# First keys without the padding waits, heads in two halves, and twelve low parts by an adding DMA: a two-block fp32 network on one core

## The chip, the core and the metric

The kernel runs on one core of a Trainium2 chip. Five engines run side by side: TensorE (PE, matrix products; PEld is its weight load), VectorE (DVE), ScalarE (ACT), GpSimd (POOL) and SyncE (SP, which here only issues DMAs). They share an on-chip memory, wait for each other on semaphores, and each works through its own queue in order. TensorE writes to PSUM, eight banks of 512 fp32 columns. The metric is the device time of one execution in microseconds.

## The reference

Two transformer-like blocks over 512 positions of width 1024 (plus 16 meta tokens in front), batch 1, all in fp32. The first block mixes by retention and by sixteen stick-breaking heads, the second by a short convolution and a 31-tap convolution; each is followed by a gated feed-forward part.

```python
def stick_breaking(q, k, v):              # 16 heads of 64
    ...
        z = jnp.einsum('bhtd,bhsd->bhts', q_blk, k_pre) * scale
        ...
        log_not = jnp.where(valid, jax.nn.log_sigmoid(-z), 0.0)
        after = lax.cumsum(log_not, axis=3, reverse=True) - log_not
        a = jnp.where(valid, jnp.exp(jax.nn.log_sigmoid(z) + after), 0.0)
        outs.append(jnp.einsum('bhts,bhse->bhte', a, v_pre))

def mixer(xn, w_in, conv_a_w, conv_b_w, conv_b_bias, ln_b_gain, ln_b_bias, w_out):
    h = jnp.einsum("btd,de->bte", xn, w_in)
    b_gate, c_gate, h_a, glu_val, glu_gate = jnp.split(...)
    y_a = b_gate * causal_depthwise_conv(c_gate * h_a, conv_a_w)      # 3 taps
    g = glu_val * jax.nn.sigmoid(glu_gate)
    z = causal_depthwise_conv(g, conv_b_w) + conv_b_bias              # 31 taps
    y_b = jax.nn.silu(layer_norm(z, ln_b_gain, ln_b_bias))
    return jnp.einsum("bte,ed->btd", jnp.concatenate([y_a, y_b], axis=-1), w_out)
```

## The kernel before

Every fp32 product is made of three: an operand x is held as a rounded high part and a low part (x minus the high part), and `mm3` multiplies high by high, high by low and low by high (L497 to L499). The weights come in 140 units of 1 MB (128 x 2048 fp32), in a ring of two: SP loads unit u into `w_raw[u % 2]`, ScalarE copies it to `w_hi` (`split_hi`, L907), VectorE subtracts to get `w_lo` (`split_lo`, L1354), and TensorE waits for `w_lo_ready`. `split_hi(at, j)` and `split_lo(at, j)` are called for the unit two further on than unit j of the stage, once TensorE has done with unit j. `plan()` fixes which unit belongs to which stage. The order of work on each engine is the order of the calls in its block; nothing reorders it.

The first keys. VectorE splits units 0 and 1 (`first_split`), then scales the input and makes its low part tile by tile (`norm_split`), while TensorE runs small filler products (`keep_warm`) and then the keys and queries of the first head pair (`key_strip`). When the last low part stands, GpSimd zeroes the unused halves of the padded keys (four memsets, L476) and four more tiles (L479), counted by `keys_padded`. VectorE waits for all eight before `key_lo` and `query_lo`; TensorE then makes the scores of head 0 (`scores`, `meta_scores`).

The heads. For each of 16 heads: `scores` on TensorE, a softplus on ScalarE and VectorE that ends in `sp_hi`, `sp_lo` (column half 1, 768 columns of key blocks 1 to 3, is made before half 0, 512 columns of block 0), `logs` on TensorE (L641, cumulative sums over both), exponentials and `a_hi` on ScalarE, `a_lo` on VectorE, and `outputs` on TensorE. Between them TensorE works on weight units; in quads 1 to 3 VectorE also adds output strips to `acc` (`add_up`, L1522).

The convolution stage. Units of conv_b (4), conv_a (6), w_out2_a (2) and w_out2_b (2) pass through the ring. ScalarE takes each strip out of PSUM and then calls `split_hi`. VectorE runs 124 steps of the long convolution (`taps(n)`, 31 for each of four tiles, L1360, the first two of a pair L1869), the short convolution, and ten `split_lo` in between at fixed places. After w_out2_a TensorE runs 45 filler products, sums z over the channels (`mean`, L887), VectorE centres z, ScalarE squares it, TensorE sums the squares (`var`, L891), and so on to `y2`, which w_out2_b needs.

## Time and profile before

| | us |
|---|---|
| median of 3 runs | 1925.59 (1923.89 to 1926.1) |
| the profiled execution, its own time | 1925.76 |
| its span in the profile | 1924.0 |
| TensorE busy | 1868.7 (97%) |
| VectorE busy | 1139.6 (59%) |
| ScalarE busy | 708.6 (37%) |
| weight loads, 1 MB each, issue to landing | 4.9 (median) |

The profile is one execution. A row of the timeline gives when a run of like instructions starts, how long it takes in all, the engine, the line, the tiles, and in brackets how long the engine stood still before it and what released it. Times of the profile are counted from the start of the span. What lies outside the span is 1.76 us.

### The profile page before, as it was taken

The numbers are of one execution on the slowest core, as the hardware profiler recorded it, in microseconds if no ns is written. First come the engines' busy times: TensorE is split into PE (matmuls) and PEld (weight loads), VectorE is DVE, ScalarE is ACT, GpSimd is POOL, SyncE is SP. The second block draws the span as 40 slices with busy tenths as digits, with TensorE's granted clock in tenths as the row PEclk, the third lists the DMA queues.
The fourth block names the chain that finished last, engine by engine and source line by source line (L and its number), as shares of the span: only waits on it lengthen the run. The fifth ranks groups of instructions, "written<-read, shape, count | busy, mean of one in ns | idle before, by whom it ended". The sixth has DMA issues, their size and how long they took to land.

```text
span 1924.0 us, 24895 instructions
## 1 busy us (share of the span) xinstructions
PE 1868.7 (97%) x9978; PEld 1601.9 (83%) x9978; DVE 1139.6 (59%) x1418; ACT 708.6 (37%) x841; POOL 21.9 (1%) x21
## 2 busy tenths in 40 slices
PE   7999999899999999999899999999999999999996
PEld 7898989789898888988788888887998688888885
DVE  5566665653645647356565454547699765554546
ACT  4666666533323332333342222224323542222222
POOL 1000000010000000000000000000000000000000
PEclk8999999999999999999999999999999999999998
DMA  4011111122222222112513222221121212232221
GB/s 178 23 66 45 66 44 44 44 99 99 66 88 76 87 81 82 67 66 72 194 44 110 87 98 98 90 107 66 67 88 66 110 35 97 90 106 87 98 99 44
DMA packets 23186, 157.45 MB, mean 82 GB/s; under 512 B 2512, under 2 KB 2768, under 8 KB 5072
## 3 DMA queue, kind: packets, MB, share of 16 engines
q1 hardware_dynamic: 23120, 156.51, 23.3%
q8 instruction: 49, 0.80, 0.2%
q14 instruction: 17, 0.14, 0.0%
HBM read 154.40 MB, written 2.10 MB: 81 GB/s over the span
## 4 chain that ended last, share of the span: by engine, by line
PE 85%; DVE 8%; ACT 3%; issue 2%; DMA 1%; POOL 0%; SPq 0%; DVEq 0%; ACTq 0%; POOLq 0%
PE psum L497 27%; PE psum L498 26%; PE psum L499 26%; PE psum L641 2%; DVE z L1360 2%; PE psum L598 1%; DMA w_raw<-in_units 1%; DVE normed L1360 1%; ACT w_hi L907 1%; DVE w_lo L1354 1%; DVE h L1387 1%; ACT std L907 0%; PE psum L662 0%; PE psum L559 0%; DVE normed L1404 0%
## 5 line engine op out<-in xcount | busy, mean ns | idle before, releaser
L497 PE MATMUL psum<-X_hi,w_hi 128*128 128x512 f32 (+1 forms) x1632 | 588.7, 361 | 3.8 <-DVE w_lo L1354 2.3
L498 PE MATMUL psum<-X_lo,w_hi 128*128 128x512 f32 (+1 forms) x1632 | 582.1, 357 | 0.0
L499 PE MATMUL psum<-X_hi,w_lo 128*128 128x512 f32 (+1 forms) x1632 | 582.1, 357 | 0.0
L1354 DVE TENSOR_TENSOR w_lo<-w_raw,w_hi 128x2048 fp32r<-128x2048 f32 x134 | 306.9, 2291 | 155.8 <-ACT w_hi L907 155.8
L907 ACT ACTIVATE w_hi<-w_raw 128x2048 fp32r<-128x2048 f32 x134 | 255.8, 1909 | 373.5 <-PE psum L499 366.0
L497 PEld LDWEIGHTS psum<-X_hi,w_hi 128*128 128x128 f32 x1632 | 307.0, 188 | 52.2 <-issue 4.8
L498 PEld LDWEIGHTS psum<-X_lo,w_hi 128*128 128x128 f32 x1632 | 307.5, 188 | 45.2 <-issue 2.4
L499 PEld LDWEIGHTS psum<-X_hi,w_lo 128*128 128x128 f32 x1632 | 307.1, 188 | 44.2
L1522 DVE TENSOR_TENSOR acc<-acc,psum 128x512 f32<-128x512 f32 x216 | 142.1, 685 | 61.3 <-PE psum L499 60.8
L497 PE MATMUL psum<-M_hi,w_hi 128*128 128x512 f32 x352 | 137.0, 389 | 0.0
L498 PE MATMUL psum<-M_lo,w_hi 128*128 128x512 f32 x352 | 137.0, 389 | 0.0
L499 PE MATMUL psum<-M_hi,w_lo 128*128 128x512 f32 x352 | 137.0, 389 | 0.0
L497 PE MATMUL psum<-w_hi,X_hi 128*128 128x256 f32 x384 | 108.9, 283 | 0.0
L498 PE MATMUL psum<-w_lo,X_hi 128*128 128x256 f32 x384 | 108.7, 283 | 0.0
L499 PE MATMUL psum<-w_hi,X_lo 128*128 128x256 f32 x384 | 108.7, 283 | 0.0
L1802 DVE TENSOR_TENSOR gate_in<-psum,std 128x512 f32<-128x512 f32 x44 | 30.2, 691 | 122.1 <-PE psum L499 109.0
L907 ACT ACTIVATE silu_a<-gate_in 128x512 f32<-128x512 f32 x44 | 27.6, 631 | 168.9 <-DVE gate_in L1802 168.9
L1360 DVE SCALAR_TENSOR_TENSOR z<-glu,vec,z 128x512 f32<-128x512 f32 x120 | 80.5, 750 | 0.0
L499 PEld LDWEIGHTS psum<-M_hi,w_lo 128*128 128x128 f32 x352 | 66.1, 188 | 13.7
L498 PEld LDWEIGHTS psum<-M_lo,w_hi 128*128 128x128 f32 x352 | 66.1, 188 | 13.7
L497 PEld LDWEIGHTS psum<-M_hi,w_hi 128*128 128x128 f32 x352 | 66.1, 188 | 13.7
L497 PEld LDWEIGHTS psum<-w_hi,X_hi 128*128 128x128 f32 x384 | 73.8, 192 | 1.0 <-issue 0.2
...
## 6 DMA issues: line engine op xcount, KB each, us to landing
w_raw<-in_units SPq DMA_DIRECT2D x140, 1024.0 KB, 4.9
...
h<-in_xfm SPq DMA_DIRECT2D x1, 2112.0 KB, 7.4
...
```

The costliest lines, as they stand in the source:

```text
L497: nc.tensor.matmul(dst, w2[0], x2[0], start=first, stop=False, skip_group_check=True)
L498: nc.tensor.matmul(dst, w2[0], x2[1], start=False, stop=False, skip_group_check=True)
L499: m = nc.tensor.matmul(dst, w2[1], x2[0], start=False, stop=last, skip_group_check=True)
L598: m = nc.tensor.matmul(psum[0:rows, at.bank(s) + 1, 0:256], XM[:, k, meta], y[:, k, :], start=k == 0 and y is w[0], stop=k == DT - 1 and y ...
L641: m = nc.tensor.matmul(psum[:, 4 + KEY_BANK[b], c0:c0 + KEY_LEN[b2]], cmat[:, C_TRI if b2 == b else C_ALL, :], x[:, KEY_OFF[b2]:KEY_OFF[b2 ...
L907: return nc.scalar.activation(out_, in_, f, **kw)
L1354: v.tensor_tensor(lo, w_raw[at.ring(j)][:, :], as_f32(hi), ALU.subtract).then_inc(w_lo_ready, 1)
L1360: return v.scalar_tensor_tensor(out=out_, in0=in0, scalar=scalar, in1=in1, op0=op0, op1=op1)
L1387: v.tensor_tensor(h[:, k, META:FULL], h[:, k, META:FULL], normed[:, k % 2, 0:SEQ], ALU.add)\
L1522: v.tensor_tensor(dst[:, m, :], dst[:, m, :], strip_view(at.bank(s + n), SEQ), ALU.add)\
L1802: v.tensor_tensor(gate_in[:, c, :], strip_view(at.bank(s + c), SEQ), std[:, 0:SEQ], ALU.mult)\
```

## The change

Three parts. (1) First keys: VectorE splits unit 1 after `norm_split` instead of before; `key_lo` and `query_lo` no longer wait for GpSimd; only the small copies of the meta keys (`meta_keys_of`), now behind `query_lo`, and the scores wait for the first four memsets, and TensorE waits for all eight before the first quad. (2) Heads: `logs` and `outputs` go through key blocks 1, 2, 3, 0; blocks 1 to 3 wait for `sp_lo1` (`a_lo1`) alone, block 0 for `sp_lo0` (`a_lo0`); the exponentials, `a_hi` and `a_lo` are made in the same two halves. (3) Convolution stage: the low parts of twelve units (the third unit of conv_b to the second of w_out2_b) are no longer made by VectorE. ScalarE writes minus the rounded weights into `w_lo`, and GpSimd issues a DMA that adds `w_raw` to it; TensorE and the load of the next unit in the slot wait for that DMA's landing. The taps are portioned anew, two of the four sums over z stand between the units of w_out2_a, and 45 filler products become 8 and 8. The same wait (`weights_ready`) also replaces `w_lo_ready` in `unit`, `key_strip` and the feed-forward part; a few lines that only rename steps, semaphores and arguments are left out here.

```diff
 START, N_UNITS, N_STRIPS = plan()
+ADDED = (START["conv_b"][0] + 2, START["w_out2_b"][0] + 2)
+N_ADDED = ADDED[1] - ADDED[0]
+def added(u):
+    return type(u) is int and ADDED[0] <= u < ADDED[1]
...
         return w_hi[ring][:, :], w_lo[ring][:, :]
+    def lo_added(u):
+        return w_lo_added[u % 2], 16 * ((u - ADDED[0]) // 2 + 1)
...
         constant(rot[:, :, :].rearrange("p a b -> p (a b)"), 0)
-        def load(u, slot):
+        def load(u, slot, less):
             sync.wait_ge(w_hi_ready, u - 1)
-            sync.wait_ge(w_lo_ready, u - 1)
+            if type(u) is int and added(u - 2):
+                sync.wait_ge(*lo_added(u - 2))
+            else:
+                sync.wait_ge(w_lo_ready, u - 1 - less)
...
         sync.dma_start(meta2_f[:, :, :].rearrange("p a b -> p (a b)"), meta2).then_inc(x_loaded, 16)
-        loads(START["ffn0"][0] - 2, N_UNITS)
+        loads(START["ffn0"][0] - 2, ADDED[0] + 2)
+        for u in range(ADDED[0] + 2, N_UNITS):
+            load(u, u % 2, N_ADDED)
...
         for n in range(2):
+            if n:
+                for u in range(*ADDED):
+                    pool.wait_ge(w_neg_ready, u - ADDED[0] + 1)
+                    pool.dma_start(as_f32(w_lo[u % 2][:, :]), w_raw[u % 2][:, :], accum_op=ALU.add)\
+                        .then_inc(w_lo_added[u % 2], 16)
...
                 m.then_inc(*sig)
+        def weights_ready(at, j):
+            u = at.unit(j)
+            if added(u):
+                pe.wait_ge(w_hi_ready, u + 1)
+                pe.wait_ge(*lo_added(u))
+            else:
+                pe.wait_ge(w_lo_ready, u + 1 - (N_ADDED if at.u0 >= ADDED[1] else 0))
...
         def value_strip(at, j, s, half, meta):
-            pe.wait_ge(w_lo_ready, at.unit(j) + 1)
+            weights_ready(at, j)
...
         def logs(g):
-            pe.wait_ge(hd_dve.sem, hd_dve.at("sp_lo0", g))
-            for b in range(BLOCKS):
+            for b in (1, 2, 3, 0):
+                pe.wait_ge(hd_dve.sem, hd_dve.at("sp_lo1" if b else "sp_lo0", g))
...
                                              start=False, stop=False, skip_group_check=True)
-            m.then_inc(*hd_pe.step("logs"))
+                if b in (3, 0):
+                    m.then_inc(*hd_pe.step("logs1" if b else "logs0"))
...
         def outputs(t, r, g, p):
-            pe.wait_ge(hd_dve.sem, hd_dve.at("a_lo", g))
+            pe.wait_ge(hd_dve.sem, hd_dve.at("a_lo1", g))
                 pe.wait_ge(y_out, p)
-            for b in range(BLOCKS):
+            for b in (1, 2, 3, 0):
+                if b == 0:
+                    pe.wait_ge(hd_dve.sem, hd_dve.at("a_lo0", g))
                     split(a_hi, a_lo, ALL, slice(KEY_OFF[b], KEY_OFF[b] + KEY_LEN[b])),
-                    r == 0 and b == 0, False)
+                    r == 0 and b == 1, False)
...
         pe.wait_ge(quad_ready, 4)
-        pe.wait_ge(keys_padded, 8)
+        pe.wait_ge(keys_padded, 4)
         meta_scores(0, 0)
+        pe.wait_ge(keys_padded, 8)
...
         at = Place("w_out2_a")
-        for j in range(2):
-            unit(at, j, 4 * j, "R", SEQ, y2, None, counted(y2_ready, 0) if j == 0 else None)
-        keep_warm(45)
-        for t in range(CT):
+        def mean_of(t):
                              skip_group_check=True).then_inc(*c_pe.step(f"mean{t}"))
+        for j in range(2):
+            unit(at, j, 4 * j, "R", SEQ, y2, None, counted(y2_ready, 0) if j == 0 else None)
+            if j == 0:
+                mean_of(0)
+                mean_of(1)
+        keep_warm(8)
+        mean_of(2)
+        mean_of(3)
+        keep_warm(8)
...
             act.wait_ge(w_loaded[at.ring(j)], 16 * (at.loads(j) + 1))
+            u = at.unit(j)
+            if type(u) is int and added(u + 2):
+                a(w_lo[at.ring(j)][:, :], w_raw[at.ring(j)][:, :], ACT.Copy, scale=-1.0).then_inc(w_neg_ready, 1)
...
             a(sp_all_hi[:, :], sp[:, 0:SEQ], ACT.Copy).then_inc(*hd_act.step("all_hi"))
-            act.wait_ge(hd_pe.sem, hd_pe.at("logs", g))
-            for n, (bank, off, w) in enumerate(PARTS):
-                a(a_f[:, off:off + w], psum[:, 4 + bank, 0:w], ACT.Exp).then_inc(*hd_act.step(f"a_part{n}"))
-            act.wait_ge(hd_act.sem, hd_act.at("a_part2", g))
-            a(a_hi[:, :], a_f[:, :], ACT.Copy).then_inc(*hd_act.step("a_hi"))
+            for half, cols, parts in ((1, H1, (1, 2)), (0, H0, (0,))):
+                act.wait_ge(hd_pe.sem, hd_pe.at(f"logs{half}", g))
+                for n in parts:
+                    bank, off, w = PARTS[n]
+                    a(a_f[:, off:off + w], psum[:, 4 + bank, 0:w], ACT.Exp).then_inc(*hd_act.step(f"a_part{n}"))
+                act.wait_ge(hd_act.sem, hd_act.at(f"a_part{parts[-1]}", g))
+                a(a_hi[:, cols], a_f[:, cols], ACT.Copy).then_inc(*hd_act.step(f"a_hi{half}"))
...
         query_hi(0, at, 1)
+        act.wait_ge(w_lo_ready, 2)
...
             split_lo(at, 1)
-        for u in range(2):
-            first_split(u)
+        first_split(0)
         norm_split(0, 0, FULL, "pre_mix")
+        first_split(1)
...
                 .then_inc(*hd_dve.step("all_lo"))
-            dve.wait_ge(hd_act.sem, hd_act.at("a_hi", g))
-            v.tensor_tensor(a_lo[:, :], a_f[:, :], as_f32(a_hi[:, :]), ALU.subtract)\
-                .then_inc(*hd_dve.step("a_lo"))
+            for half, cols in ((1, slice(SEQ, PACKED)), (0, slice(0, SEQ))):
+                dve.wait_ge(hd_act.sem, hd_act.at(f"a_hi{half}", g))
+                v.tensor_tensor(a_lo[:, cols], a_f[:, cols], as_f32(a_hi[:, cols]), ALU.subtract)\
+                    .then_inc(*hd_dve.step(f"a_lo{half}"))
...
             ins.then_inc(strip_free, 1)
-            if not (type(p) is int and p == 0):
-                dve.wait_ge(mk_pe.sem, mk_pe.at("m_scores", p - 1))
+            if type(p) is int and p == 0:
+                return
+            dve.wait_ge(mk_pe.sem, mk_pe.at("m_scores", p - 1))
+            meta_keys_of(t, at, s)
+        def meta_keys_of(t, at, s):
...
         dve.wait_ge(quad_ready, 4)
-        dve.wait_ge(keys_padded, 8)
         query_lo(0, at, 1, 0)
+        dve.wait_ge(keys_padded, 4)
+        meta_keys_of(0, at, 0)
...
                     .then_inc(y2_ready, 1)
-        b, ca = Place("conv_b"), Place("conv_a")
-        split_lo(b, 0)
-        split_lo(b, 1)
         dve.wait_ge(c_dve.sem, c_dve.at("glu1"))
-        taps(11)
-        split_lo(b, 2)
-        taps(13)
-        split_lo(b, 3)
+        taps(31)
         gated_linear(1)
-        taps(11)
-        split_lo(ca, 0)
-        taps(13)
-        split_lo(ca, 1)
+        taps(29)
         short_conv(0)
-        taps(5)
+        taps(2)
+        dve.wait_ge(c_dve.sem, c_dve.at("glu3"))
+        taps(6)
         y_a(0)
-        taps(3)
+        taps(2)
         y_a_lo(0)
-        split_lo(ca, 2)
-        taps(6)
-        dve.wait_ge(c_dve.sem, c_dve.at("glu3"))
-        split_lo(ca, 3)
-        taps(13)
-        split_lo(ca, 4)
+        taps(26)
         short_conv(1)
-        taps(4)
+        taps(8)
         y_a(1)
-        taps(1)
+        taps(2)
         y_a_lo(1)
-        split_lo(ca, 5)
             stt(z[:, t, :], psum[:, 4, :], -1.0 / WB, z[:, t, :], ALU.mult, ALU.add).then_inc(*c_dve.step(f"zc{t}"))
-        for j in range(2):
-            split_lo(Place("w_out2_a"), j)
```

VectorE at the first keys, before (`first_split(1)`, then `norm_split` to its last tile, then the first keys and queries):

```order
L1394 CAST w_hi<-w_raw 128x2048 [waits w_loaded1]
L1396 TENSOR_TENSOR w_lo<-w_raw,w_hi 128x2048 [waits w_hi_ready]
L1360 SCALAR_TENSOR_TENSOR normed<-h,vec,std 128x528 [waits x_in2,x_in3,x_in1,std_ready,x_in0,vec_in]
...
L1369 TENSOR_TENSOR X_lo<-normed,X_hi 128x528 [waits x_hi_ready] x2
L1481 TENSOR_TENSOR K_lo<-psum,K_hi 64x528 [waits keys_padded,qk_act,quad_ready,consts_in]
L1481 TENSOR_TENSOR K_lo<-psum,K_hi 64x528 [waits qk_act]
L1488 CAST KM_hi<-K_hi 128x64 [waits strip_free]
L1490 CAST KM_lo<-K_lo 128x64
L1360 SCALAR_TENSOR_TENSOR Q_lo<-psum,Q_hi 128x512 [waits qk_act]
```

and after:

```order
L1445 TENSOR_TENSOR w_lo<-w_raw,w_hi 128x2048 [waits w_hi_ready]
L1409 SCALAR_TENSOR_TENSOR normed<-h,vec,std 128x528 [waits x_in2,x_in3,x_in1,std_ready,x_in0,vec_in]
...
L1418 TENSOR_TENSOR X_lo<-normed,X_hi 128x528 [waits x_hi_ready] x2
L1443 CAST w_hi<-w_raw 128x2048 [waits w_loaded1]
L1445 TENSOR_TENSOR w_lo<-w_raw,w_hi 128x2048 [waits w_hi_ready]
L1531 TENSOR_TENSOR K_lo<-psum,K_hi 64x528 [waits qk_act,quad_ready,consts_in]
L1531 TENSOR_TENSOR K_lo<-psum,K_hi 64x528 [waits qk_act]
L1409 SCALAR_TENSOR_TENSOR Q_lo<-psum,Q_hi 128x512 [waits qk_act]
L1542 CAST KM_hi<-K_hi 128x64 [waits strip_free,keys_padded]
L1544 CAST KM_lo<-K_lo 128x64
```

The two instructions of `first_split(1)` moved from ahead of `norm_split` to behind it, the wait for `keys_padded` from the keys to the meta copies, and these behind the queries.

VectorE in the second half of the convolution stage, from the last tap group of the middle portion to the centring of z (`z<-psum`), before:

```order
L1360 SCALAR_TENSOR_TENSOR z<-glu,vec,z 128x512 [waits conv_step] x11
L1354 TENSOR_TENSOR w_lo<-w_raw,w_hi 128x2048 [waits w_hi_ready]
L1887 TENSOR_TENSOR u_in<-c_in,u_in 128x528 [waits strip_free]
...
L1360 SCALAR_TENSOR_TENSOR z<-glu,vec,z 128x512 [waits conv_step] x4
L1906 TENSOR_TENSOR c_in<-c_in,b_in 128x512 [waits c_dve,strip_free]
L1906 TENSOR_TENSOR c_in<-c_in,b_in 128x512 [waits c_dve]
L1360 SCALAR_TENSOR_TENSOR z<-glu,vec,z 128x512 [waits conv_step]
L1913 TENSOR_TENSOR y_lo<-c_in,y_hi 128x512 [waits c_act] x2
L1354 TENSOR_TENSOR w_lo<-w_raw,w_hi 128x2048 [waits w_hi_ready]
L1360 SCALAR_TENSOR_TENSOR z<-glu,vec,z 128x512 [waits conv_step] x44
L1360 SCALAR_TENSOR_TENSOR z<-psum,z 128x512 [waits c_pe]
```

and after:

```order
L1409 SCALAR_TENSOR_TENSOR z<-glu,vec,z 128x512 [waits conv_step] x26
L1942 TENSOR_TENSOR u_in<-c_in,u_in 128x528 [waits strip_free]
...
L1409 SCALAR_TENSOR_TENSOR z<-glu,vec,z 128x512 [waits conv_step] x8
L1961 TENSOR_TENSOR c_in<-c_in,b_in 128x512 [waits c_dve,strip_free]
L1961 TENSOR_TENSOR c_in<-c_in,b_in 128x512 [waits c_dve]
L1409 SCALAR_TENSOR_TENSOR z<-glu,vec,z 128x512 [waits conv_step] x2
L1968 TENSOR_TENSOR y_lo<-c_in,y_hi 128x512 [waits c_act] x2
L1409 SCALAR_TENSOR_TENSOR z<-glu,vec,z 128x512 [waits conv_step] x18
L1409 SCALAR_TENSOR_TENSOR z<-psum,z 128x512 [waits c_pe]
```

The low parts of the weights are gone from between the taps, and 18 taps stand where 44 stood.

TensorE from the end of a w_out2_a unit to w_out2_b (`psum<-z,ones` are the sums over z, `psum<-ones` the filler), before:

```order
L499 MATMUL psum<-y_hi,w_lo 128x512
L569 MATMUL psum<-ones 128x128 x45
L887 MATMUL psum<-z,ones 128x512 [waits conv_step] x4
L891 MATMUL psum<-sq,ones 128x512 [waits c_act] x4
L569 MATMUL psum<-ones 128x128 x30
L497 MATMUL psum<-y_hi,w_hi 128x512 [waits strip_free,y2_ready,w_lo_ready]
```

and after:

```order
L523 MATMUL psum<-y_hi,w_lo 128x512
L920 MATMUL psum<-z,ones 128x512 [waits conv_step] x2
L521 MATMUL psum<-y_hi,w_hi 128x512 [waits strip_free,w_lo_added0,w_hi_ready]
...
L523 MATMUL psum<-y_hi,w_lo 128x512
L601 MATMUL psum<-ones 128x128 x8
L920 MATMUL psum<-z,ones 128x512 [waits conv_step] x2
L601 MATMUL psum<-ones 128x128 x8
L934 MATMUL psum<-sq,ones 128x512 [waits c_act] x4
L601 MATMUL psum<-ones 128x128 x30
L521 MATMUL psum<-y_hi,w_hi 128x512 [waits strip_free,y2_ready,w_lo_added1,w_hi_ready]
```

Two sums moved ahead of the second unit; the waits for the weights now name the DMA's semaphore.

## Rows read from the trace of the kernel before

**Rows 1.** The page, part 1: busy us, share of span, instructions by engine.

```profile
PE 1868.7 (97%) x9978; PEld 1601.9 (83%) x9978; DVE 1139.6 (59%) x1418; ACT 708.6 (37%) x841; POOL 21.9 (1%) x21
```

**Rows 2.** Timeline, VectorE, first keys: start us, us, engine, line, op, [idle before].

```profile
19.12 1.44 DVE L1360 SCALAR_TENSOR_TENSOR normed<-h,vec,std 128x528 f32<-128x528 f32 x2
...
29.13 1.50 DVE L1369 TENSOR_TENSOR X_lo<-normed,X_hi 128x528 fp32r<-128x528 f32 x2
36.85 1.42 DVE L1481 TENSOR_TENSOR K_lo<-psum,K_hi 64x528 fp32r<-64x528 f32 x2 [6.22 <-POOL m_lo L479]
38.31 1.96 DVE L1488 CAST KM_hi<-K_hi 128x64 fp32r<-128x64 f32 x1
...
77.02 0.20 DVE L1488 CAST KM_hi<-K_hi 128x64 fp32r<-128x64 f32 x1
```

**Rows 3.** Timeline, ScalarE, GpSimd and TensorE, first keys.

```profile
16.19 0.65 ACT L907 ACTIVATE std<-std 128x528 f32<-128x528 f32 x1
...
33.66 0.60 ACT L907 ACTIVATE Q_hi<-psum 128x512 fp32r<-128x512 f32 x1
...
33.80 0.97 POOL L476 MEMSET K_lo<- 64x1056 f32 x1
...
15.25 5.52 PE L569 MATMUL psum<-ones 128*128 128x128 f32 x48
21.45 0.36 PE L497 MATMUL psum<-X_hi,w_hi 128*128 128x264 f32 x1 [0.67 <-DVE X_lo L1369]
...
41.18 0.77 PE L497 MATMUL psum<-Q_hi,K_hi 128*128 128x512 f32 x1 [8.12 <-DVE Q_lo L1360]
```

**Rows 4.** Windows: us, busy us PE PEld DVE ACT POOL, granted clock, DMA.

```profile
46.00:47.00 1.00, 1.00 (x5) 0.74 (x4) 0.00 (x0) 1.00 (x3) 0.00 (x0) 0.67 1.04 442
...
924.20:927.60 3.40, 1.11 (x5) 0.64 (x4) 2.77 (x2) 0.60 (x1) 0.00 (x0) 0.96 0.04 17
```

**Rows 5.** Waits of TensorE, whole span: us in total, times, longest.

```profile
PE psum L641 <- DVE sp_lo L1438: 4.2, 3, 1.4
```

**Rows 6.** Timeline, TensorE and VectorE, third head of quad 1.

```profile
177.91 0.50 PE L641 MATMUL psum<-sp_hi,cmat 128*128 128x512 f32 x1 [1.39 <-DVE sp_lo L1438]
187.34 0.44 PE L662 MATMUL psum<-sp_all_hi,cmat 128*64 128x512 f32 x1 [0.32 <-DVE sp_all_lo L1450]
...
183.79 0.69 DVE L1522 TENSOR_TENSOR acc<-acc,psum 128x512 f32<-128x512 f32 x1 [0.61 <-PE psum L499]
```

**Rows 7.** Timeline, VectorE and TensorE, convolution stage.

```profile
1384.23 2.29 DVE L1354 TENSOR_TENSOR w_lo<-w_raw,w_hi 128x2048 fp32r<-128x2048 f32 x1 [1.15 <-ACT w_hi L907]
...
1469.06 29.25 DVE L1360 SCALAR_TENSOR_TENSOR z<-glu,vec,z 128x512 f32<-128x512 f32 x44
...
1485.17 10.21 PE L569 MATMUL psum<-ones 128*128 128x128 f32 x90
1495.22 1.88 PE L887 MATMUL psum<-z,ones 128*128 128x512 f32 x4
```

**Rows 8.** Timeline, ScalarE, convolution stage.

```profile
1370.61 1.91 ACT L907 ACTIVATE w_hi<-w_raw 128x2048 fp32r<-128x2048 f32 x1
...
1381.78 0.61 ACT L907 ACTIVATE conv_sig<-psum 128x528 f32<-128x528 f32 x1 [5.00 <-PE psum L499]
...
1430.19 1.23 ACT L907 ACTIVATE y_hi<-c_in 128x512 fp32r<-128x512 f32 x2 [1.89 <-DVE c_in L1906]
...
1439.38 0.61 ACT L907 ACTIVATE c_in<-psum 128x528 f32<-128x528 f32 x1 [4.72 <-PE psum L499]
...
1487.78 1.28 ACT L963 ACT_TABLE_LOAD   x1
1500.44 1.23 ACT L907 ACTIVATE sq<-z 128x512 f32<-128x512 f32 x2 [11.38 <-DVE z L1360]
```

**Rows 9.** DMA issues of the program: count, KB each, median us to landing.

```profile
w_raw<-in_units SPq DMA_DIRECT2D x140, 1024.0 KB, 4.9
...
h<-in_xfm SPq DMA_DIRECT2D x1, 2112.0 KB, 7.4
```

22 lines of the change are left out of this document (12 added, 10 removed).

## The prediction, on record before the changed kernel was run

> **What bounds the kernel now.** I read the page first, then TensorE's waits, then the timelines around the three places that the diff touches. The page says who is the bound: TensorE is busy 97% of the span, VectorE 59%, ScalarE 37% [rows 1]. So work taken from VectorE is worth something only where TensorE stands still for VectorE, or runs filler in place of work. In the timelines the reader is to look at the brackets and at filler. Three such places are in reach. At the first keys TensorE stands still for 8.12 us until 41.18 [rows 3]. In the head pairs it waits three times for `sp_lo`, 4.2 us in all [rows 5]. After the convolution it finishes real work at 1485.2 and runs 10.2 us of filler, since VectorE's taps run on to 1498.3 [rows 7]; ScalarE waits 11.38 us for that, until 1500.44 [rows 8].
>
> **Part 1, the first keys.** `norm_split` begins at 19.12, behind `first_split(1)` [rows 2]. What it needs, std, is there at 16.19 + 0.65 = 16.84 [rows 3], so it moves up by about 2.2 us and its last low part ends at 28.4 instead of 30.6. TensorE's filler ends at 15.25 + 5.52 = 20.77 and the first key product waits 0.67 more for X_lo [rows 3]: from then on filler and not X_lo is late, so the key and query products end 0.65 earlier, at about 32.4. ScalarE's Q_hi, which ended at 34.26 [rows 3], ends at 33.6.
>
> The split of unit 1 now stands behind: its two instructions took 3.5 us (15.65 to 19.2, the gap in front of 19.12), so they run from 28.4 to 31.9 and end before the first K_hi is there (32.35). Then K_lo twice, 0.7 each, the second ending at 33.7, and Q_lo, 0.7, ends at 34.4. The four pads of the keys ended at 34.77 [rows 3]; GpSimd starts on the last X_lo, so 2.2 us earlier: 32.5, or 33.8 if its first memset waits for the 1.2 us copy of `first_split(1)`. Both lie before 34.4. The 6.22 us wait for GpSimd ahead of K_lo and the 1.96 us of the meta copy ahead of Q_lo [rows 2] are gone from the path. The scores start at about 34.5 instead of 41.18: 6.7 us.
>
> Then the clock. The trace shows half the full clock (1.2 instead of 2.4 GHz) while the scores run, until about 46.7: the second from 46 to 47 has a mean of 0.67 [rows 4]. From 41.18 to 46.7 are 5.5 us at half clock, 2.75 of them lost. TensorE had stood still for over 8 us. Now it stands still for 2.1 us only, and I take the clock as staying full: 2.3 us more (the same products end at 37.8 instead of 46.8). The counter-case is in the trace too: a stretch of 3.4 us with 1.11 us of work, before 927.6 [rows 4], was followed by half clock. Sum: 9.0 us with full clock, 6.5 to 7.3 if it falls. The load of unit 3 now waits for the later split of unit 1, until 31.9; with 4.9 us [rows 9] it lands at 37, long before ScalarE wants it (past 50). The wait for all eight memsets ends at about 36, behind it 37.8.
>
> The copies (CAST) and the memsets. KM_hi took 1.96 us beside GpSimd's memset of `acc`, and 0.20 at 77.02 without one [rows 2]: they hold each other up. The 1.2 us copy of unit 1 now meets the first pad; if it is the one that waits (0.97 us), Q_lo comes 0.7 later. That is in the range. The Trainium skill (SBUF — State Buffer, Who interferes with whom) says that the two engines share a port pair that one instruction holds for its whole length; the trace agrees.
>
> **Part 2, the heads.** A wait of 1.39 us [rows 6] ends when both halves of `sp_lo` stand. Half 0 takes 0.6 to 0.7 us of VectorE after half 1; `logs` on blocks 1 to 3 has 1.4 us of work before it wants half 0. So each wait shrinks by 0.7. The next wait of TensorE, 0.32 at 187.34, is on a chain of VectorE whose `acc` addition at 183.79 waited for TensorE itself [rows 6]; it moves along by 0.6. Three waits (quads 1 to 3), 0.6 each: 1.8 us. The additional instructions (one copy on ScalarE, one subtraction on VectorE per head) cost 0.1 us each, 16 times, and lie beside TensorE's weight units; no wait of TensorE over 0.2 us names `a_lo`. If they were on the path it would be a loss of 1.6, which the range holds.
>
> **Part 3, the convolution stage, if the DMAs are in time.** Ten splits of 2.29 us [rows 7] leave VectorE before the end of the taps, and so do seven short waits like the 1.15 ahead of one. Laid out again (taps 0.67 each, each block behind the strip that it waits for), the last tap ends at about 1478.5 instead of 1498.3. VectorE is then no longer late. What is late next: TensorE. It ends w_out2_a at 1485.2, plus two sums moved in between, 0.94 each [rows 7]: 1487.1. Then 8 fillers of 0.23, two sums, and z can be centred at 1490.9. But ScalarE is later still: its last strip moves by 1.9, and the negated copy adds 1.9 ahead of w_hi and the table load. That load ended at 1487.78 + 1.28 = 1489.06 [rows 8], and now ends at 1492.85. The squares started at 1500.44 and start at 1492.85: 7.6 us. From the squares on the chain is the same; the two splits that VectorE ran in it were hidden. The negated copy (1.9) in front of w_hi also delays one strip of w_out2_a by 0.2.
>
> **The adding DMA.** No row shows one. Its time T runs from the end of the negated copy to the release of TensorE. What T may be: ScalarE starts on a unit at 1370.61, TensorE has done with the next at 1381.7, just ahead of ScalarE's take at 1381.78 [rows 8]. 11.1 less 1.9 leaves 9.2 us. The tightest is the fifth unit of conv_a: ScalarE makes y_hi first, until 1431.4 (some 1 us earlier once VectorE is not behind), the copy ends at 1432.1, and TensorE wants the unit at 1439.3 [rows 8]: 7.2 us. One more has 8.4 us, the other six or seven about 9.2; the last two units have time to spare.
>
> Bounds of T: from below a plain load, 4.9 us [rows 9]. A 2112 KB load takes 7.4, so 2.3 of it are fixed and 1 MB takes 2.5. An addition reads two operands for one that it writes: 2.3 + 5.0 = 7.3, and GpSimd has to issue it, which I put at up to 1 us, from the 1 us that its small memsets take [rows 3]. From above: nothing in the trace excludes that the adding is several times slower; I take two loads behind each other with a third for the adding, 14 us. I choose 8, since all of its parts but the adding itself come from rows. Then one unit is 0.8 us late, and part 3 brings 7.6 - 0.2 - 0.8 = 6.6.
>
> The Trainium skill bears on it in two places. DMA: Bandwidth & Descriptors (Anatomy of one DMA — SWDGE) gives about 2.0 us plus bytes / 436 GB/s, and Collectives: The Full Stack (The bandwidth ceiling) says that a reducing transfer runs at half the rate of a copy, because of the second read and not because of the adding. Together an estimate of 6.8 us, by which no unit would be late and the sum 0.8 us better; no row here shows it.
>
> **Sum:** 9.0 + 1.8 + 6.6 = 17.4 us. Against the profiled execution's 1925.76 (0.17 above the median of 1925.59): 1908.4. The three parts lie behind each other on TensorE's path, so they add.
>
> **Rivals.** (a) The clock falls at the first keys after all: 1.7 to 2.5 us less, 1910.5. For it: the row before 927.6. Against it: 2.1 us of standstill instead of 8. (b) The DMA takes 9 to 11 us. At 10 the tightest unit is 2.8 late, the next 1.6, the others 0.8 each, some 10 in all: 1918. Every further us costs 10. Nothing speaks against it but the estimate above. (c) Slower: the DMA takes over 11.2 us, the point at which its lateness, some 22 us, eats 18.2 of gain and 4 more. TensorE then waits at each of ten units of the stage, and TensorE's own wait for `w_lo_added` takes the place of VectorE's taps as the bound. At 13 us: 5.8 + 4.6 + 8 x 3.8 = 41 us late, 1949. For it: no row shows an addition by DMA, and its descriptors are written by GpSimd, which VectorE's copies hold up [rows 2]. Against it: 2.5 us of data for 1 MB leaves room for four passes. (d) The edits do little of what they say: the head halves gain nothing, since VectorE's chain is late anyway, or the squares are bound elsewhere: 1911 to 1914.
>
> **Numbers.** Forecast 0.50 (own range 1904 to 1912), (a) 0.15, (b) 0.15, (c) 0.13, (d) 0.07. The range 1904 to 1921 takes in the forecast, (a), (d) and most of (b); (c) and the rest of (b) stay out, some 0.18. A measurement of this kernel tells 0.2% (3.9 us) from no change. Faster by more: all but (c) and the slow end of (b), 0.83. Within: 0.04, the slow end of (b) and the start of (c). Slower: 0.13.
>
> **What would show it.** Part 1: scores start near 34.5, the row with the 8.12 us bracket is down to about 2, and the granted clock is 1.0 there. Part 2: the brackets on the first `logs` product of a third head near 0.7. Part 3: the last tap ends more than 5 us before TensorE's second pair of sums; squares start about 7.5 us earlier against the start of the stage; TensorE's waits on `w_lo` in the stage are under 1 us in all. It is wrong if the DMA's issue-to-landing is over 9 us, with a bracket of the same size ahead of each unit's first product; or if ScalarE, with 3.8 us of weight copies per unit, is late for strips.

## The result, and the profile after

The changed kernel takes 1907.9 us (median of 4 runs, 1907.39 to 1908.21), the kernel before in the same session 1925.11 (1923.89 to 1926.1). The ratio is 0.9911, with a 95% interval of 0.9893 to 0.9928: 17.2 us faster (the interval allows 13.9 to 20.6), where 17.4 were forecast (1908.4). The profiled execution has a span of 1906.4 against 1924.0.

The page of the changed kernel, its line on the engines (the answer to [rows 1]) and its two lines on DMA issues (median us from issue to landing at the end; the second is new):

```profile
PE 1860.9 (98%) x9920; PEld 1593.0 (84%) x9920; DVE 1113.3 (58%) x1422; ACT 733.2 (38%) x869; POOL 33.5 (2%) x33
...
w_raw<-in_units SPq DMA_DIRECT2D x140, 1024.0 KB, 4.8
w_lo<-w_raw POOLq DMA_DIRECT2D x12, 1024.0 KB, 6.9
```

**The first keys** (the answer to [rows 2, 3]), timeline of the changed kernel:

```profile
15.84 5.52 PE L601 MATMUL psum<-ones 128*128 128x128 f32 x48
17.55 1.45 DVE L1409 SCALAR_TENSOR_TENSOR normed<-h,vec,std 128x528 f32<-128x528 f32 x2 [1.80 <-ACT std L950]
28.99 1.22 DVE L1443 CAST w_hi<-w_raw 128x2048 fp32r<-128x2048 f32 x1
29.13 2.00 POOL L495 MEMSET K_hi<- 64x1056 f32 x1 [28.18 <-DVE X_lo L1418]
31.19 0.98 POOL L495 MEMSET K_lo<- 64x1056 f32 x1
32.79 1.42 DVE L1531 TENSOR_TENSOR K_lo<-psum,K_hi 64x528 fp32r<-64x528 f32 x2 [0.26 <-ACT K_hi L950]
34.25 0.69 DVE L1409 SCALAR_TENSOR_TENSOR Q_lo<-psum,Q_hi 128x512 fp32r<-128x512 f32 x1
34.85 0.18 DVE L1542 CAST KM_hi<-K_hi 128x64 fp32r<-128x64 f32 x1
35.08 0.47 PE L521 MATMUL psum<-Q_hi,K_hi 128*128 128x512 f32 x1 [2.37 <-POOL VM_lo L498]
55.83 0.50 PE L521 MATMUL psum<-Q_hi,K_hi 128*128 128x512 f32 x1 [0.49 <-DVE V_lo L1555]
```

`first_split(1)` now runs at 28.99 and `norm_split` follows std. The 6.22 us ahead of K_lo have become 0.26, the meta copy of 1.96 us stands behind Q_lo and takes 0.18, and the scores start at 35.08 instead of 41.18. The bracket of 2.37 names a GpSimd memset; that memset, at 34.64, is the sixth of the eight, and the wait asks for four. The last instruction that it can be is Q_lo, which ends at 34.94.

The granted clock there (the answer to [rows 4]; columns: stretch, its length, busy time of PE, PEld, DVE, ACT, POOL, granted clock, DMA share, GB/s):

```profile
36.00:37.00 1.00, 1.00 (x10) 1.00 (x9) 1.00 (x1) 0.00 (x0) 0.94 (x2) 1.00 0.94 393
37.00:38.00 1.00, 1.00 (x10) 0.81 (x9) 1.00 (x1) 0.34 (x1) 1.00 (x1) 1.00 0.08 16
```

**The heads.** TensorE's waits on `sp_lo` (in all, how often, the longest), the answer to [rows 5]:

```profile
PE psum L673 <- DVE sp_lo L1487: 2.4, 3, 0.8
```

They were 4.2, three times, 1.4. The 0.32 us waits on `sp_all_lo` [rows 6] are gone. In their place stand three pauses that are too short for a bracket: at 174.30, 257.52 and 340.68 a product of a weight unit starts 0.51 to 0.52 behind the one in front of it, where 0.23 is the rhythm. The kernel before has none of them. The same pause in `halves_only` (part 2 alone, below) stands ahead of its second row here:

```profile
181.64 0.39 PE L499 MATMUL psum<-Y_hi,w_lo 128*128 128x512 f32 x1
182.15 0.50 PE L497 MATMUL psum<-Y_hi,w_hi 128*128 128x512 f32 x1
```

There VectorE starts two `acc` additions at 181.43, 1.33 us in all, and TensorE goes on about when the first of them ends; in the kernel before, the second of these additions waited for TensorE [rows 6].

**Behind the convolution** (the answer to [rows 7, 8]), timeline of the changed kernel:

```profile
1456.28 12.02 DVE L1409 SCALAR_TENSOR_TENSOR z<-glu,vec,z 128x512 f32<-128x512 f32 x18
1477.80 1.90 ACT L950 ACTIVATE w_lo<-w_raw 128x2048 fp32r<-128x2048 f32 x1
1479.60 1.90 ACT L950 ACTIVATE w_hi<-w_raw 128x2048 fp32r<-128x2048 f32 x1
1480.61 1.95 PE L601 MATMUL psum<-ones 128*128 128x128 f32 x16
1480.81 2.48 DVE L1409 SCALAR_TENSOR_TENSOR z<-psum,z 128x512 f32<-128x512 f32 x4 [12.52 <-PE psum L920]
1481.52 1.28 ACT L1009 ACT_TABLE_LOAD   x1
1482.81 1.15 ACT L950 ACTIVATE sq<-z 128x512 f32<-128x512 f32 x2
1483.50 3.89 PE L934 MATMUL psum<-sq,ones 128*128 128x512 f32 x8 [0.94 <-ACT sq L950]
```

VectorE's last tap ends at 1468.3 and it then waits 12.52 us for the sums: it was the last here and is now the first. ScalarE has no bracket from 1477.80 to the squares: two copies and a table load set their start. The fillers are down from 10.21 us to twice 1.95.

**Where the 17.6 us of span come from.** I cut TensorE's queue at the same five events in every kernel: the first score product, the first product behind a wait for V_lo (55.83 here), the one behind the wait of 3.58 on Y_lo, the first product of the convolution stage (bracket 0.66), and the first sum of squares in it. The first and the last stretch of the table reach to the ends of the span.

| stretch, us | before | after | gain |
|---|---|---|---|
| start to scores | 41.18 | 35.08 | 6.10 |
| scores to the wait on V_lo | 23.26 | 20.75 | 2.51 |
| to the wait on Y_lo | 316.12 | 314.06 | 2.06 |
| to the convolution stage (no edit) | 965.55 | 965.95 | -0.40 |
| convolution stage to the squares' sums | 155.02 | 147.66 | 7.36 |
| to the end (no edit that moves it) | 422.87 | 422.90 | -0.03 |

### The profile page after: what moved, and what is told of

It reads as the page before. It is cut to its first block, busy times and chain, and to the rows that moved or that the text cites. A ratio compares the mean times of both kernels' runs of the same rounds, so it can differ in the third digit from the quotient of the medians.

```text
span 1906.4 us, 24709 instructions
## 1 busy us (share of the span) xinstructions
PE 1860.9 (98%) x9920; PEld 1593.0 (84%) x9920; DVE 1113.3 (58%) x1422; ACT 733.2 (38%) x869; POOL 33.5 (2%) x33
## 4 chain that ended last, share of the span: by engine, by line
PE 88%; DVE 6%; ACT 3%; issue 2%; DMA 0%; POOL 0%; SPq 0%; DVEq 0%; ACTq 0%; POOLq 0%
PE psum L521 28%; PE psum L523 27%; PE psum L522 27%; PE psum L673 2%; PE psum L630 1%; ACT w_hi L950 1%; DVE normed L1409 1%; DVE h L1436 1%; DMA w_raw<-in_units 0%; PE psum L583 0%; DVE w_lo L1403 0%; ACT std L950 0%; PE psum L601 0%; ACT m_f L950 0%; PE psum L695 0%
## 5 line engine op out<-in xcount | busy, mean ns | idle before, releaser
L1403 DVE TENSOR_TENSOR w_lo<-w_raw,w_hi 128x2048 fp32r<-128x2048 f32 x122 | 279.4, 2290 | 133.2 <-ACT w_hi L950 133.2
```

The costliest lines, as they stand in the source:

```text
L1403: v.tensor_tensor(lo, w_raw[at.ring(j)][:, :], as_f32(hi), ALU.subtract).then_inc(w_lo_ready, 1)
```

## The experiments

### Each part alone

`first_keys_only` is the kernel before with part 1 alone, `halves_only` with part 2, `adding_dma_only` with part 3 (the diffs are those pieces of the change above).

> The kernel before with part 1 alone (split of unit 1 behind norm_split, keys and queries without the padding wait, meta copies behind the queries). Theory: the scores of head 0 start about 6 us earlier and run at full clock, together 8.6 to 9.0 us, so about 1916.3 against 1925.1. Rival (only the earlier start counts, the clock's part is given back elsewhere): 6.1 us, 1919.0.

> The kernel before with part 2 alone (heads in two halves). Theory: the three waits for sp_lo of 1.39 us fall to 0.8, and the wait behind them does not take it back: 1.8 to 2.0 us, about 1923.2. Rival (VectorE's chain is late anyway): the waits of 0.32 on sp_all_lo grow to 0.9 and the gain is 0.3 us or less.

> The kernel before with part 3 alone (twelve low parts by the adding DMA, taps portioned anew, sums and fillers moved). Theory: the squares of z start 7.3 to 7.6 us earlier, 1917.7. The three parts add up to 17.2 to 18.4 us if they are independent. Rival (part 3 gained less, and part of its gain in the joined kernel came from a shifted clock): under 6 us.

| | median us | ratio, 95% | start | V_lo | Y_lo | no edit | stage |
|---|---|---|---|---|---|---|---|
| before (its profile) | 1925.38 | | 41.18 | 23.26 | 316.12 | 965.55 | 155.02 |
| first_keys_only | 1916.11 | 0.9956 (0.9941 to 0.9971) | 34.78 | 20.73 | 316.16 | 963.91 | 154.96 |
| halves_only | 1924.01 | 0.9994 (0.9985 to 1.0003) | 40.98 | 22.69 | 314.08 | 966.21 | 155.01 |
| adding_dma_only | 1917.0 | 0.9961 (0.9945 to 0.9976) | 41.69 | 22.20 | 316.09 | 963.75 | 147.67 |
| all three | 1907.9 | 0.9911 (0.9893 to 0.9928) | 35.08 | 20.75 | 314.06 | 965.95 | 147.66 |

(The last five columns are the stretches of the table above, in the profiled execution of each.) Behind the start, the stretch that a part changes has the same length alone as in all three together, to 0.02 us (20.73 and 20.75, 314.08 and 314.06, 147.67 and 147.66), and outside the clock's stretch at V_lo those of the other parts stay within 0.06. So the parts do add. The medians alone don't say it as well: they give 9.27 + 1.37 + 8.38 = 19.0 for 17.2. The spans of the single profiles are 10.6, 1.9 and 9.7 shorter, 22.2 in all for 17.6, and their stretches show where the 4.6 too many lie: 3.2 in the stretch that no edit touches and 1.65 in the clock's stretch at V_lo, which was shorter than before in the two kernels without part 1 as well (22.69 and 22.20); the other stretches take 0.25 back. Over all fourteen profiles of this case the untouched stretch took from 963.00 to 967.91 us. The two rows of windows below are from it, of `first_keys_only` (963.91) and of `split_ahead_filled` (967.91, further down). First the one, then the other:

```profile
920.00:930.00 10.00, 10.00 (x45) 8.28 (x45) 4.62 (x6) 3.07 (x3) 0.00 (x0) 1.00 0.54 203
```

```profile
920.00:930.00 10.00, 9.99 (x31) 8.00 (x32) 5.94 (x7) 3.62 (x4) 0.00 (x0) 0.69 0.51 171
```

In ten us the one has the full clock and the other 0.69 of it. The mean granted clock differs between executions of one kernel too: the four of `first_keys_only` have 0.995, 0.995, 0.993 and 0.993, with spans of 1913.4, 1912.6, 1915.6 and 1915.1. So differences of 1 to 3 us are read from stretches and not from medians. `halves_only` is the example: its interval includes 1, and its trace has the 2.04 us (316.12 to 314.08), with 0.79 ahead of a third head:

```profile
176.23 0.44 PE L641 MATMUL psum<-sp_hi,cmat 128*128 128x384 f32 x1 [0.79 <-DVE sp_lo L1443]
```

The column "start" moves by chance, and in a way that shows what part 1 did. Where the padding wait stands (before, `halves_only`, `adding_dma_only`, `filler_at_first_keys`), the scores start 29.09 to 29.13 us behind the landing of the first weights, here in the kernel before:

```profile
12.05 1.23 DVE L1394 CAST w_hi<-w_raw 128x2048 fp32r<-128x2048 f32 x1 [12.05 <-DMA w_raw<-in_units]
```

In the eight kernels with the whole of part 1 they start 17.67 to 17.70 behind the end of std, and no longer at a fixed distance from that landing (21.4 to 23.6). Part 1 has put another event in the lead.

### The clock at the first keys

`filler_at_first_keys` is the kernel before with filler in the gap of 8.12 us:

```diff
         key_strip(at, 0, 0, counted(x_lo_ready, 0), True)
+        keep_warm(32)
```

> The kernel before with 32 filler products behind the first keys, inside TensorE's 8.12 us wait, and nothing else changed. Theory: the scores start where they did, near 41.2, but at full clock; the clock's part of part 1 alone, 2.3 to 2.75 us, about 1922.6. Rival (the clock would have come back by itself, or the scores' chain on VectorE and ScalarE hides it): 0.

1923.66 us, ratio 0.9993 (0.9984 to 1.0002). The ratio can't be told from 1, but the timeline shows the effect:

```profile
33.16 7.30 PE L569 MATMUL psum<-ones 128*128 128x128 f32 x64
41.44 0.47 PE L497 MATMUL psum<-Q_hi,K_hi 128*128 128x512 f32 x1 [0.97 <-DVE Q_lo L1361]
62.16 0.51 PE L497 MATMUL psum<-Q_hi,K_hi 128*128 128x512 f32 x1 [0.49 <-DVE V_lo L1502]
```

The scores start as late as before (41.44), and the stretch behind them takes 20.72 instead of 23.26. That is the changed kernel's 20.75: the 2.5 us are the clock's, apart from the 6.1 of the earlier start.

`split_ahead` is the changed kernel with `first_split(1)` put back in front of `norm_split`:

> The changed kernel with the split of unit 1 ahead of norm_split again; the padding waits stay away. Theory: TensorE's filler hides most of norm_split's move, and the four pads end at 34.8: the scores start 0.6 to 0.7 us later than in the changed kernel (35.1), 1908.5. Rival (norm_split's move is worth its 2.2 us): 1910.1.

1910.19 us (1907.18 to 1910.74, 5 runs), ratio 0.9923 (0.9909 to 0.9936). The median lies at the rival's number, yet the scores start at 35.21, 0.13 later than with the split behind. Part of that is chance: in the changed kernel's profile std ended at 17.41, 0.58 later than here (16.83). With std at 16.83 the changed kernel's scores would start at 34.50 (17.67 behind it), so here the order of the split costs 0.7 us. The rest is the clock. It is 0.71 from 36 to 37 and 0.59 from 39 to 40, and between them, in the same view as above:

```profile
37.00:38.00 1.00, 1.00 (x7) 1.00 (x6) 1.00 (x1) 0.00 (x0) 1.00 (x1) 0.50 0.06 16
38.00:39.00 1.00, 1.00 (x5) 0.82 (x5) 0.17 (x1) 0.17 (x1) 1.00 (x1) 0.50 0.00 0
```

The stretch to the wait on V_lo took 22.31 instead of 20.75. This is rival (a) of the prediction, and it isn't tied to the order of the split: of nine profiles of different kernels with part 1 and without filler in this place, three have it (`split_ahead`, `dma_2us_later`, `ten_adds_less_filler`: 22.31, 22.32, 22.30), and six have 20.73 to 20.75. All nine stand still for the same 2.4 us ahead of the scores. A fall costs 1.56 us (22.31 against 20.75).

`split_ahead_filled` puts filler into the 2.37 us as well:

```diff
         key_strip(at, 0, 0, counted(x_lo_ready, 0), True)
+        keep_warm(16)
```

> split_ahead with 16 fillers (1.84 us at full clock) behind the first key and query products, in the gap of 2.37 us in which TensorE waits for Q_lo. split_ahead started its scores at 35.21, as the changed kernel did, but its granted clock was at half from 36.7 to 39.6 and it lost 1.6 us there (the wait behind the first head began 1.69 later); its five times went from 1907.18 to 1910.74. Theory (the standstill ahead of the scores, with the 0.46 us ahead of the first products, is what lets the clock fall): filled, the clock is 1.00 from 34 to 42 in the profile, the scores start at 35.2 and the span is about 1906.8, the times 1907 to 1908.8. Rival (the clock falls by the phase of other work, a few us later or earlier, whatever stands in the gap): half clock somewhere before 42 again, span about 1908.4. Filler in front of the queue could also delay the scores by up to 0.3 us.

1911.58 us (1909.85 to 1912.46), ratio 0.9933 (0.9916 to 0.9949). Slower than without filler, and both accounts missed. Timeline:

```profile
33.33 3.73 PE L601 MATMUL psum<-ones 128*128 128x128 f32 x32
36.81 0.48 PE L521 MATMUL psum<-Q_hi,K_hi 128*128 128x512 f32 x1
57.56 0.51 PE L521 MATMUL psum<-Q_hi,K_hi 128*128 128x512 f32 x1 [0.49 <-DVE V_lo L1556]
```

One call of 16 issues 32 products, 3.73 us and not the 1.84 that I wrote. They overran the gap, and the scores began 1.60 later than in `split_ahead`. Of that 0.61 is the first weights' later landing (12.44 against 11.83), and 1.0 the filler. The clock did stay full from 34 to 42, and the stretch behind took 20.75: the filler gave back 1.56 and cost 1.0. What made this profile 2.2 us longer all the same lies elsewhere: 1.7 in the untouched stretch (967.91 against 966.25, the row with 0.69 above) and 0.5 in the convolution stage, where TensorE waited 0.50 for an adding DMA that took 7.4. That filler can hold the clock there is shown; that it pays isn't: 0.6 in this place is less than the runs scatter, and `split_ahead` has the fall in its profile but not in every run (1907.18 to 1910.74).

### What a later adding DMA costs

The changed kernel, with two, four or six memsets of a spare tile in front of each adding DMA:

```diff
                     pool.wait_ge(w_neg_ready, u - ADDED[0] + 1)
+                    for k in range(2):          # 4, 6
+                        pool.wait_ge(keys_padded, 8 + 2 * (u - ADDED[0]) + k)
+                        nc.gpsimd.memset(rot[:, :, :], 0.0).then_inc(keys_padded, 1)
                     pool.dma_start(as_f32(w_lo[u % 2][:, :]), w_raw[u % 2][:, :], accum_op=ALU.add)\
```

> The changed kernel with two memsets of a tile no longer in use (about 1.03 us each) on GpSimd ahead of each adding DMA, so that each low part comes 2.06 us later. With T = 7.2 us (0.3 to the issue, 6.9 to the landing) plus 2.06 = 9.3: by the table of budgets (7.2 for one unit, 8.4 for one, 9.2 for six) 2.1 + 0.9 + 0.6, some 3.6 us slower than the changed kernel, about 1911.5. Rival (the budgets are not what counts, each of the ten units is late by what is added): 20 us slower. Other rival (there is more room than thought): 0.

> The same with four memsets, 4.12 us later, T = 11.3: 4.1 + 2.9 + 6 x 2.1 + 1.2 + 1.6, some 22 us slower than the changed kernel, about 1930, and slower than the kernel before. Rival (slack grows along with the lateness, since the loads and ScalarE's takes move too): under 12 us.

> The changed kernel with six memsets of 1.0 us in front of each adding DMA, so that each comes 6.3 us later. With 2 of them the stretch from the first product of the convolution stage to the squares was 4.1 us longer than in the changed kernel, with 4 of them 15.6 us. With 4, the waits of TensorE came at every other unit: 0.15, 1.42, then 2.32, 0, 2.95, 0. Theory (two slots: the unit after a late one has the lateness as extra time, because its own add was started by the end of the product before the late one, so a pair of units costs its lateness once): per unit half of what its add is late. Then 2 us more cost about 1 us for each of 11 units, 10 to 12 in all: 15.6 + 11 = 26.6 over the changed kernel, span 1933, time 1934.5. Rival (each unit pays the whole of its lateness, as the prediction's rival (c) reckoned, and 4 us were cheap only since the budgets of single units were larger): 2 us more cost 2.1 us for each of ten or eleven units, 22 in all: span 1944, time 1945.5.

| memsets | from negated copy to landing (medians) | median us | ratio, 95% | stage | over "none" |
|---|---|---|---|---|---|
| none | 7.2 | 1907.9 | 0.9911 (0.9893 to 0.9928) | 147.66 | |
| 2 | 9.1 | 1912.48 | 0.9936 (0.9921 to 0.9951) | 151.76 | 4.10 |
| 4 | 11.1 | 1923.61 | 0.9995 (0.9986 to 1.0005) | 163.30 | 15.64 |
| 6 | 13.2 | 1939.29 | 1.0079 (1.0062 to 1.0096) | 179.46 | 31.80 |

"Stage" is the stretch from its first product to the squares' sums in the profile. With four memsets (two rows of GpSimd, then TensorE's brackets at the first product of units that follow each other):

```profile
1361.26 4.28 POOL L513 MEMSET rot<- 128x1056 f32 x4 [7.00 <-ACT w_lo L953]
1365.49 0.86 POOL L514 DMA_DIRECT2D w_lo<-w_raw  x1
...
1360.35 0.36 PE L524 MATMUL psum<-X_hi,w_hi 128*128 128x264 f32 x1 [1.60 <-issue]
1372.42 0.36 PE L524 MATMUL psum<-X_hi,w_hi 128*128 128x264 f32 x1 [0.15 <-issue]
1385.75 0.36 PE L524 MATMUL psum<-X_hi,w_hi 128*128 128x264 f32 x1 [1.42 <-issue]
1399.98 0.36 PE L524 MATMUL psum<-X_hi,w_hi 128*128 128x264 f32 x1 [2.32 <-issue]
...
1427.25 0.36 PE L524 MATMUL psum<-X_hi,w_hi 128*128 128x264 f32 x1 [2.95 <-issue]
```

Unit by unit TensorE waits 1.60, 0.15, 1.42, 2.32, none, 2.95, none, 1.81, 1.23 and 1.04, 12.5 us in all (0.89 of the 1.23 stands in the changed kernel too, there for `b_in`). A large wait has a small one or none next to it. The reason is the ring of two. The add of unit k+1 is started when TensorE has done with unit k-1. If unit k was late by L, then k+1's add was started L ahead of where it would stand in an even sequence, and k+1 waits L less. So a pair of units pays once, and the waits come to 11.6 more than in the changed kernel and not to the 22 that a full wait at each unit would give; my number for the kernel, near 1930, was too high for that. The stage is 15.6 longer; an estimate for the clock is further down.

With six the same rule gave 1934.5, and the other 1945.5. Measured: 1939.3, between them. The waits obey the rule. From six memsets (timeline, and windows with the columns as above):

```profile
1362.43 0.36 PE L524 MATMUL psum<-X_hi,w_hi 128*128 128x264 f32 x1 [3.67 <-issue]
...
1451.61 0.56 PE L524 MATMUL psum<-X_hi,w_hi 128*128 128x264 f32 x1 [5.97 <-issue]
```

```profile
1440.00:1455.00 15.00, 9.03 (x62) 8.85 (x61) 15.00 (x24) 4.90 (x5) 11.79 (x13) 0.81 0.50 122
```

Strictly every other unit waits: 3.67, then 4.07 at 1391.36 and 4.05 at 1420.51, 5.97, and 4.98 at 1481.41, in all 22.7 us against 12.5 with four memsets. 10.2 more is what "once per pair" predicts (10 to 12). But the stage is 16.2 longer, not 10.2. The clock accounts for the rest: ahead of and behind these waits the granted clock was 0.79 to 0.99 in eight of nine windows of 15 us from 1350 to 1485, while with four memsets two of nine were below 1.0 (0.89) and with none none. TensorE's busy time in each window times the share of the clock that is missing there makes 9.2 us with six memsets and 2.8 with four, an estimate of 6.4 more. So the last 2 us of delay cost 10.2 in waits and 6.0 on top of them.

### What ends last behind the convolution

`filler_45_kept` is the changed kernel with `keep_warm(45)` in place of the first `keep_warm(8)`.

> The changed kernel with 45 filler products in place of the first 8 behind w_out2_a. 37 x 0.227 = 8.4 us more of filler; ScalarE is ready 2 us behind the centring, so the squares start 6.4 us later: about 1914.3. Rival (the gain lies in VectorE's earlier taps, the filler ends early anyway): 0.

1915.65 us, ratio 0.9953 (0.9938 to 0.9969): 7.8 more than the changed kernel, and its stage 7.8 longer (155.49). Of that 0.65 is a wait for an adding DMA at 1429.91 (which took 7.5 from issue to landing, and 6.9 in the changed kernel), so about 7.2 are the filler's, where 6.4 were expected. Its timeline:

```profile
1477.96 10.21 PE L601 MATMUL psum<-ones 128*128 128x128 f32 x90
1482.38 1.28 ACT L1009 ACT_TABLE_LOAD   x1
1489.93 2.48 DVE L1409 SCALAR_TENSOR_TENSOR z<-psum,z 128x512 f32<-128x512 f32 x4 [20.80 <-PE psum L920]
1490.65 1.23 ACT L950 ACTIVATE sq<-z 128x512 f32<-128x512 f32 x2 [7.00 <-DVE z L1409]
```

ScalarE's table load ends at 1483.7 and it then waits 7.00 us for a centring that waits for sums behind filler. So part 3 gains nothing without the shorter filler: the twelve moved splits free VectorE, but TensorE's own filler would have kept the place. No run has the shorter filler alone. The trace of the kernel before speaks against a gain from it, since there the last sums over z waited for VectorE's last tap, behind all filler:

```profile
1497.70 1.98 PE L887 MATMUL psum<-z,ones 128*128 128x512 f32 x4 [0.60 <-DVE z L1360]
```

In the changed kernel ScalarE ended last. `ten_adds` lets VectorE make the low parts of both w_out2_b units again (ten adds are left), and `ten_adds_less_filler` drops the first `keep_warm(8)` besides and has VectorE cast one high part:

```diff
-ADDED = (START["conv_b"][0] + 2, START["w_out2_b"][0] + 2)
+ADDED = (START["conv_b"][0] + 2, START["w_out2_b"][0])
...
+        split_lo(Place("w_out2_a"), 0)     # before the mean's wait
...
+        split_lo(Place("w_out2_a"), 1)     # behind the centring
```

```diff
-        keep_warm(8)
         mean_of(2)
...
-            split_hi(at, j)
+            if j == 0:
+                split_hi(at, j)
...
+        at = Place("w_out2_a")
+        dve.wait_ge(w_loaded[at.ring(1)], 16 * (at.loads(1) + 1))
+        strips(at, 7)
+        v.tensor_copy(w_hi[at.ring(1)][:, :], w_raw[at.ring(1)][:, :]).then_inc(w_hi_ready, 1)
```

> The changed kernel, but the low parts of the two units of w_out2_b are again made by VectorE (2.29 us each: one ahead of the mean's wait, one behind the centring), so ScalarE no longer negates them and ten adds are left. In the changed kernel the squares started at 1482.81, behind a table load that ended at 1482.80; ahead of it stood two copies of the first unit of w_out2_b (1477.80 and 1479.60, 1.9 each). Theory (behind the convolution it is ScalarE that ends last): one 1.9 us copy less, and the table load would end at 1481.0; then the centring is late, which the last sum on z releases: it started at 1480.81 and gives z of the first group at about 1481.4. So squares at about 1481.45, 1.35 us earlier: span 1905.0, time 1906.6. Rival (the wait for the sums of z is last anyway and the table load only ends beside it): squares unchanged, span 1906.4, time 1907.9. A VectorE that comes too late with the second low part would show as a bracket on w_out2_b's first product behind 1520.

> The same as ten_adds, without the first eight fillers ahead of the sums of z (0.9 to 1.8 us of TensorE by 0.115 to 0.23 each), and with VectorE casting the high part of the second unit of w_out2_b's first use, so that ScalarE has another 1.9 us less ahead of its table load. Theory (ScalarE and TensorE end within 1.4 us of each other there, so both have to be shortened): squares about 3.1 us before 1482.81, span 1903.3, time 1904.8, some 3 us or 0.16% under the changed kernel. Rival (VectorE's last taps, which ended at 1468.3, or the chain mean, centring, squares sets it): not more than ten_adds, 1906.6. If the missing filler lets the clock fall behind it, the granted clock between 1478 and 1500 goes under 1.0 and the time is above ten_adds.

`ten_adds`: 1906.8 us (1906.02 to 1907.14), ratio 0.991 (0.9893 to 0.9926). `ten_adds_less_filler`: 1904.2 us (1902.76 to 1906.55), ratio 0.9901 (0.9885 to 0.9918). From the first product of the stage to the squares' sums they take 146.56 and 144.75, against 147.66: 1.1 and 2.9 us less, where 1.35 and 3.1 were expected. First `ten_adds`:

```profile
1480.74 1.95 PE L601 MATMUL psum<-ones 128*128 128x128 f32 x16
1481.67 1.23 ACT L950 ACTIVATE sq<-z 128x512 f32<-128x512 f32 x2 [0.54 <-DVE z L1409]
1482.53 3.79 PE L934 MATMUL psum<-sq,ones 128*128 128x512 f32 x8
```

Then `ten_adds_less_filler`:

```profile
1476.50 1.95 PE L601 MATMUL psum<-ones 128*128 128x128 f32 x16
1476.70 2.48 DVE L1409 SCALAR_TENSOR_TENSOR z<-psum,z 128x512 f32<-128x512 f32 x4 [0.42 <-PE psum L920]
1477.43 1.23 ACT L949 ACTIVATE sq<-z 128x512 f32<-128x512 f32 x2 [0.54 <-DVE z L1409]
1478.29 3.79 PE L933 MATMUL psum<-sq,ones 128*128 128x512 f32 x8
```

In both the squares now wait for the centring and no longer for the table, and the sums of squares have no bracket: they start where the second filler of 1.95 us ends. That filler is what took the missing 0.2. `ten_adds_less_filler` has the shortest time of all kernels here (its profile has the clock's fall at the first keys and still a span of 1901.1, helped by the shortest untouched stretch of all, 963.00 against 965.95); that it beats the changed kernel by more than the runs scatter is shown by the stretches, not by the medians of two sessions.

## Why the prediction was right

**Part 1 (9.0 forecast, 8.6 measured).** The start: 6.7 forecast, 6.10 measured. By chance std ended 0.57 later in this profile than in that of before (17.41 against 16.84). With the 17.67 that the changed kernel takes from there, the std of before would give 34.51, which is 6.67 under 41.18. The steps came as written: std releases `norm_split`, the order of the split is worth well under its 2.2 us since filler and the products hide most, and what remains on the path is K_lo, K_lo, Q_lo. One size was off on the way: GpSimd's first memset took 2.00 us beside the copy of `first_split(1)`, not 0.97; the copy kept its 1.22, so it was the memset that waited, and the pads were not on the path. The clock: 2.3 forecast, 2.51 measured, and `filler_at_first_keys` separates it. Here the reason was weaker than the number: that 2.4 us of standstill leave the clock full holds in six profiles out of nine. Rival (a), which I gave 0.15, came in three of the nine, at 1.56 us each where 1.7 to 2.5 were written.

**Part 2 (1.8 forecast, 2.06 measured from the wait on V_lo to that on Y_lo).** Three waits went from 1.39 to 0.79, 0.6 each, and the 0.32 on `sp_all_lo` went too, 2.8 us in all. That is more than the 2.06, because the three new pauses of 0.28 to 0.29 take 0.86 back. I had written that the chain behind `sp_all_lo` moves along by 0.6 and keeps its wait; it lost the wait, and a pause at an `acc` addition came in. The sum fits, and two small terms that it didn't have cancel in part. Whether the additional small instructions have a share in the new pauses was not tried.

**Part 3 (6.6 forecast, 7.36 measured).** The squares were to be bound by ScalarE's copies and its table load, and they are: no bracket from 1477.80 to 1482.81. The term that was mis-sized is T, the time of the adding DMA: 8 chosen, 7.2 measured from the end of the negated copy to the landing, of it 0.3 to the issue and 6.9 behind it. With 8 the tightest unit would have been 0.8 late; it came out at the 7.2 that this unit can bear. (The 2.3 us that I called fixed and the 2.5 for 1 MB are 2.55 and 2.35 by the two loads of [rows 9]; the sum that I took from them, 7.3, hardly moves.) The unit that follows `y_hi` was negated at 1419.93, its DMA issued at 1422.13, and the strips behind it came 0.2 later than their rhythm. 7.6 - 0.2 = 7.4 would have been the sum. The last tap ended 132.5 us behind the stage's first product, 1478.6 in the times of before, where 1478.5 was written. That the tightest unit was in time is no rule: in two of the six other kernels without added memsets, `split_ahead_filled` and `filler_45_kept`, that unit's DMA took 7.4 and 7.5 from issue to landing instead of 6.9, and TensorE waited 0.50 and 0.65 for it. The Trainium skill (DMA: Bandwidth & Descriptors, Anatomy of one DMA — SWDGE, with Collectives: The Full Stack, The bandwidth ceiling) led to an estimate of 6.8 and "no unit late, 0.8 better"; the trace agrees, with 6.8 at least, 6.9 in the median and 7.4 at most.

**The rivals (b) and (c)** were about a T that didn't come, and the three kernels with later DMAs show what they were worth. At T = 9.1 the budgets of (b) leave the tightest unit 1.9 late and the one with 8.4 us 0.7; the stage came out 4.1 longer. TensorE waited 0.75 at the second of them and 0.73 at the tightest, which comes right behind it and had the first wait as additional time. The largest wait, 1.95, stands at a unit that can bear 9.2: its DMA alone took 9.0 us from issue to landing (issued at 1388.74), and the same DMA took 9.0 in the kernel with four memsets. These three waits fit the budgets as I had read them; what I had left out is that single DMAs land late. At T = 11.2 (c) had 22 us of lateness, 4 more than the gain; at 11.1 the stage is 15.6 longer and the ratio is 0.9995. Beyond it I had 1949 at 13 us, and 1939.3 came at 13.2. The step that failed is "every further us costs 10": each unit was charged with its whole lateness, and the ring of two charges a pair once, about 5 a us, to which the clock adds some 3 when the waits get long (both from four memsets to six). It didn't bear on the forecast, since no unit was late enough.

**The sum.** 17.4 against 17.2, with terms off by -0.6, +0.2, +0.3 and +0.8, and -0.4 from a stretch in which nothing was changed. In spans it is 17.6, and the interval of the ratio is 3.4 us wide to either side. That the total fits to 0.2 us is partly luck.
